# A two-block transformer kernel: second attention's queries and output projection for 258 of 272 tokens, index queries for 256 with both activation halves in one matmul

## What is computed

```
T = N_META + S                                  # 16 + 256
q, k, v, qi, ki, wi = split(rms_norm(h) @ w_in) # layer 0; qi: 8 index heads of 64, wi: 8 weights
score = sum_h wi[h] * relu(qi[h] @ ki.T)        # which 64 keys a token attends to
h = h + attention(q, top 64 keys by score) @ w_o ; h = h + conv_ffn(rms_norm(h))
kv = rms_norm(h) @ w_kv_b ; q = rms_norm(h) @ w_q_b         # layer 1
h = h + rms_norm(attn(q1, k1, v) - lam * attn(q2, k2, v)) @ w_o_b
h = h + conv_ffn(rms_norm(h))                   # convolution over the token and the 2 before it
first stack's result: h[:, 16:272]
```

## Time and profile before

| | us |
|---|---|
| median of 3 runs | 1297.96 |
| lowest and highest of them | 1296.43, 1303.09 |
| the profiled execution's own time | 1296.1 |
| its span, first to last instruction | 1294.3 |
| TensorE matmuls busy | 1269.0 (98% of the span) |
| VectorE busy | 980.1 (76%) |
| ScalarE busy | 669.2 (52%) |
| GpSimd busy | 493.9 (38%) |

### The profile page before, as it was taken

The page is one execution under the profiler, slowest core; times in us unless marked ns, Lnnn a source line. Parts: engine busy times, 40 slices in busy tenths (PEclk is TensorE's granted clock), DMA queues, the critical chain, the costliest instruction groups (busy, mean ns, idle before and its releaser), DMA issues.

```text
span 1294.3 us, 26981 instructions
## 1 busy us (share of the span) xinstructions
PE 1269.0 (98%) x8902; PEld 1176.9 (91%) x8902; DVE 980.1 (76%) x1568; ACT 669.2 (52%) x1103; POOL 493.9 (38%) x454
## 2 busy tenths in 40 slices
PE   7999999999999999999999999999999999999998
PEld 6989999999999989999888898888888988888887
DVE  5686899975666668999765687799866876999553
ACT  5445555554555555656544455355444565455442
POOL 1043465541212225555321032299611102799222
PEclk9999999999999999999999999999999999999999
DMA  8731556566633316666666565666666542666762
GB/s 219 157 99 50 167 172 181 167 175 175 182 108 107 99 50 176 183 178 194 174 198 219 150 176 161 188 181 189 192 195 195 148 139 83 180 194 193 208 188 79
DMA packets 403204, 209.20 MB, mean 162 GB/s; under 512 B 20553, under 2 KB 397681, under 8 KB 403105
## 3 DMA queue, kind: packets, MB, share of 16 engines
q1 hardware_dynamic: 402016, 205.37, 55.4%
q0 software_dynamic: 784, 2.51, 0.9%
q10 hardware_dynamic: 320, 0.21, 0.1%
HBM read 206.98 MB, written 1.27 MB: 161 GB/s over the span
## 4 chain that ended last, share of the span: by engine, by line
PE 89%; DVE 6%; issue 2%; POOL 1%; ACT 1%; DMA 0%; DVEq 0%; POOLq 0%; ACTq 0%
PE bank L621 23%; PE bank L615 15%; PE bank L617 14%; PE bank L616 14%; PE bank L622 12%; DVE w_lo L2077 2%; PE bank L758 1%; PE bank L1180 1%; PE bank L1182 1%; PE bank L1181 1%; PE bank L745 1%; PE bank L717 1%; PE bank L1032 1%; PE bank L1019 1%; PE bank L1210 1%
## 5 line engine op out<-in xcount | busy, mean ns | idle before, releaser
L2077 DVE TENSOR_TENSOR w_lo<-w_raw,w_hi 128x1024 fp32r<-128x1024 f32 x391 | 514.4, 1328 | 28.6 <-ACT w_hi L1437 27.7
L1437 ACT ACTIVATE w_hi<-w_raw 128x1024 fp32r<-128x1024 f32 x391 | 410.7, 1053 | 128.9 <-PE bank L622 64.9
L615 PE MATMUL bank<-split_x,w_lo 128*128 128x272 f32 (+2 forms) x1128 | 328.8, 291 | 1.0 <-DVE split_x L2315 0.7
L617 PE MATMUL bank<-split_x,w_hi 128*128 128x272 f32 (+2 forms) x1128 | 321.9, 285 | 0.0
L616 PE MATMUL bank<-split_x,w_hi 128*128 128x272 f32 (+2 forms) x1128 | 321.8, 285 | 0.0
L621 PE MATMUL bank<-split_w,w_hi 128*128 128x512 f32 x880 | 307.0, 393 | 0.6 <-POOL split_w L1936 0.5
L622 PE MATMUL bank<-split_w,w_lo 128*128 128x256 f32 x880 | 246.2, 280 | 0.0
L615 PEld LDWEIGHTS bank<-split_x,w_lo 128*128 128x128 f32 x1128 | 211.4, 187 | 3.9 <-DVE split_x L2315 0.9
L616 PEld LDWEIGHTS bank<-split_x,w_hi 128*128 128x128 f32 x1128 | 211.8, 188 | 0.3
L617 PEld LDWEIGHTS bank<-split_x,w_hi 128*128 128x128 f32 x1128 | 211.5, 188 | 0.3
L621 PEld LDWEIGHTS bank<-split_w,w_hi 128*128 128x128 f32 x880 | 164.8, 187 | 38.0 <-POOL split_w L1936 0.8
(11 more groups left out here) (301 smaller groups left out, 1841.3 us busy)
## 6 DMA issues: line engine op xcount, KB each, us to landing
w_raw<-in_mlp_w_dram SPq DMA_DIRECT2D x256, 256.0 KB, 3.2
w_raw<-in_w_up_dram SPq DMA_DIRECT2D x176, 256.0 KB, 3.3
w_raw<-in_w_down_dram SPq DMA_DIRECT2D x64, 256.0 KB, 3.3
w_raw<-in_a_w_in_dram SPq DMA_DIRECT2D x64, 256.0 KB, 3.4
w_raw<-in_w_in_a_dram SPq DMA_DIRECT2D x32, 256.0 KB, 4.3
w_raw<-in_w_kv_b_dram SPq DMA_DIRECT2D x32, 256.0 KB, 3.1
w_raw<-in_a_w_out_dram SPq DMA_DIRECT2D x32, 256.0 KB, 3.2
w_raw<-in_w_down_dram SPq DMA_DIRECT2D x32, 192.0 KB, 4.1
```

The source lines that it names most:

```text
L615: pe.matmul(dst, lo, mov_h, start=first, stop=False)
L617: return pe.matmul(dst, hi, mov_h, start=False, stop=last)
L1437: act.activation(w_hi[:, n % R, :], w_raw[:, n % R, :], ACT.Copy)\
L2077: dve.tensor_tensor(w_lo[:, n % R, :], w_raw[:, n % R, :], w_hi[:, n % R, :].bitcast(F32), ALU.subtract)\
```

## The change

Two things are done. The queries of layer 1 and its output projection are computed for tokens 14 to 271 in place of 0 to 271: `q` tiles and `wo_b` tiles have 258 columns, and what reads them too. And tiles 1 to 5 of stage `in` (index queries and index weights) are computed for tokens 16 to 271 by `mm2`, with the halves of the bank joined by a reduction on VectorE where a copy stood.

```diff
+Q0 = CONV_IN[1]
...
-            def from_x(s, t0=0):
+            def from_x(s, t0=0, joint=None):
...
-                both = (lambda k: split_x[:, :, k, t0:T]) if s.name in HALVES else None
+                joint = s.name in HALVES if joint is None else joint
+                both = (lambda k: split_x[:, :, k, t0:T]) if joint else None
...
             for g in range(18):
-                product(s, None, g, m=8 if g == 5 else P, **from_x(s))
+                if 1 <= g <= 5:
+                    product(s, None, g, m=8 if g == 5 else P, **from_x(s, META, True))
+                else:
+                    product(s, None, g, **from_x(s))
...
-                    ins = mm3(stream[2 + j % 2][:, 0:T], w_lo[:, slot, w], w_hi[:, slot, w], mh[:, k, :],
-                              ml[:, k, :], k == 0, k == DT - 1)
+                    t0 = Q0 if kind == "q" else 0
+                    ins = mm3(stream[2 + j % 2][:, 0:T - t0], w_lo[:, slot, w], w_hi[:, slot, w],
+                              mh[:, k, t0:T], ml[:, k, t0:T], k == 0, k == DT - 1)
...
-                    ins = mm3(stream[(s.t0 + g) % R][:, 0:T], w_lo[:, (s.n0 + g) % R, w],
-                              w_hi[:, (s.n0 + g) % R, w], aoh[:, k, :], aol[:, k, :],
+                    ins = mm3(stream[(s.t0 + g) % R][:, 0:T - Q0], w_lo[:, (s.n0 + g) % R, w],
+                              w_hi[:, (s.n0 + g) % R, w], aoh[:, k, Q0:T], aol[:, k, Q0:T],
                               k == 0, k == DT - 1)
...
-                return dict(mh=lambda k: aoh[:, k, :], ml=lambda k: aol[:, k, :], t0=0,
+                return dict(mh=lambda k: aoh[:, k, Q0:T], ml=lambda k: aol[:, k, Q0:T], t0=Q0,
...
-                act.activation(query_b(2 * (c % 4) + 1, c // 4)[64:P, :], stream[2 + j % 2][64:P, 0:T],
-                               ACT.Copy)
+                act.activation(query_b(2 * (c % 4) + 1, c // 4)[64:P, Q0:T],
+                               stream[2 + j % 2][64:P, 0:T - Q0], ACT.Copy)
...
-                act.activation(sq_b[n % 2], stream[2 + j % 2][:, 0:T], ACT.Square).then_inc(b_sq, 1)
+                act.activation(sq_b[n % 2][:, Q0:T], stream[2 + j % 2][:, 0:T - Q0], ACT.Square)\
+                   .then_inc(b_sq, 1)
...
                     if g == 0:
-                        dst, src = ki, bk[:, 0:T]
-                    elif g < 5:
-                        dst, src = qi[:, g - 1, :], bk[:, 0:T]
+                        ins = dve.tensor_copy(ki, bk[:, 0:T])
                     else:
-                        dst, src = wi[0:8, :], bk[0:8, 0:T]
-                    dve.tensor_copy(dst, src).then_inc(S["tile_read"], 1)
+                        n = P if g < 5 else 8
+                        dst = qi[:, g - 1, META:T] if g < 5 else wi[0:8, META:T]
+                        ins = dve.tensor_reduce(dst, bk[0:n, :].rearrange("p (s t) -> p t s", s=2),
+                                                AX.X, ALU.add)
+                    ins.then_inc(S["tile_read"], 1)
...
-                    dve.tensor_copy(query_b(2 * (c % 4), c // 4)[0:64, :], bk[0:64, :])\
+                    dve.tensor_copy(query_b(2 * (c % 4), c // 4)[0:64, Q0:T], bk[0:64, 0:T - Q0])\
                        .then_inc(qb_half, 1)
...
-            residual_stage("wo_b", 0)
+            residual_stage("wo_b", Q0)
```

## The result

The changed kernel takes 1293.73 us in the median of 21 runs (1293.15 to 1295.32), the kernel before 1296.59 us in as many (1295.57 to 1303.09). The ratio is 0.9974, 95% interval 0.9967 to 0.9981: 2.5 to 4.3 us less. The forecast was 1294.3, and 3.7 us less. The sign came out, 3.7 us lies in the interval, and the change stayed within 0.5%. The medians, though, are 2.9 us apart and the profiled executions 2.6, about 1 us less than the forecast's sum, and that difference turned out to have a place and a cause. That the absolute time fell so near to 1294.3 is luck: the forecast started from a median of three runs, 1297.96, and the kernel before measured 1296.59 in 21, so the same sum would have given 1292.9.

A forecast was written before the change was run, and what follows sets the result against it. TensorE's matmul stream, busy 98% of the span at full clock, was taken as the bound. Terms 1.27 + 1.27 + 1.21 - 0.05 = 3.7 us, so 1297.96 - 3.7 = 1294.3 us; range 1290.8 to 1298.8.

The forecast's parts named there:

- The sign: Whole kernel: faster, 3.7 us less; the case of the gain kept in full had chance 0.70.
- The bound and the prices: TensorE's matmul stream bounds the changed stages; 125.8 ns per 272-column matmul, 119.2 ns per 258-column one.
- Index part: Stage `in`, index tiles: 40 steps from 377.4 to 347.2 ns, 1.21 us less, 0.05 of it not passed on.
- VectorE's wait at 48.72: Stage `in`: VectorE waits 1.16 us for a relu of tile 9, so at most 1.16 us of gain pass.
- Queries: Layer 1's query tiles: 192 matmuls from 272 to 258 columns, 1.27 us less, kept.
- Output projection: Layer 1's output projection: 192 matmuls from 272 to 258 columns, 1.27 us less, kept.
- GpSimd's reserve of 1.52 us: Behind the output projection: sum of squares ready 1.52 us before TensorE's sum; at least 0.25 us stays.
- The reductions: Stage `in`, VectorE: five reductions, 680 against 439 ns for a copy, 1.2 us more on VectorE, zero on the path.
- The remaining gap: Stage `in`: of VectorE's smaller idle time before a copy, some 0.7 us remain with the reduction.
- the second attention's last units: Stretch before layer 1's output projection: no term given, so zero change, with the granted clock high in all 40 slices.
- The rivals: The one with 2.5 us: index part lost in front of the first attention, 1295.5 us, chance 0.15.
- Two rivals: First attention: waits vanish, gain up to 9.0 us, chance 0.08; more VectorE-GpSimd meetings, 1.5 us each, chance 0.07.

The follow-up runs named there:

- layer 1 alone: Kernel before with only layer 1's queries and output projection at 258 columns, index tiles as before; 1296.47 us against 1297.74, ratio 0.9987.
- the repetition: The unaltered changed kernel measured and profiled once more beside the kernel before; 1294.9 us against 1297.34, ratio 0.998.
- the twelve idle matmuls: Changed kernel plus six idle matmuls in the wait at 457.33 and six ahead of the meta tokens' outputs; 1294.42 us against before's 1297.17, ratio 0.9974.
- the projection alone: Kernel before with only layer 1's output projection at 258 columns, queries and index tiles as before; 1296.75 us against 1297.34, ratio 0.9993.
- doubling: Changed kernel with the reductions of index tiles 1 to 4 done twice; 1294.55 us against before's 1297.34, ratio 0.9978.

## Why the prediction was right, point by point

**The bound and the prices.** TensorE's stream was the bound in all three places, and the spacings of 125.8 and 119.2 ns held in the output projection (125.8 and 119.3).

**Index part:** 1.13 us measured (S1), 1.16 forecast. The 0.05 that it took off for VectorE's wait at 48.72 were owed to nothing: that wait ended 1.39 us earlier (47.33) and was still 1.77 us long. Without them 1.21 was the price, 0.08 too much: a step took 349 ns (twenty of them from 19.86 to 26.84) in place of 347.2, and 40 x (377.4 - 349) = 1.14.

**Queries:** 1.09 in the whole change, 1.13 in layer 1 alone and in the repetition, 1.27 forecast. The term was mis-sized by 0.14 to 0.18 us, 5.7 to 5.9 ns a matmul in place of 6.6. The price came from an undisturbed stream, and these tiles are cut in two by other small matmuls. The profiles show where the rest went: the first matmul behind each such interruption takes as long in either width (402.51 to 402.74 before, 405.07 to 405.29 after; 0.22 us in the mean of all), and only the others went from 126.0 to 119.6 ns. Of 192, some 176 are others: 176 x 6.4 = 1.13 us.

**Output projection:** 1.27 forecast. Counted from its first matmul (470.53 before) to the sum of squares it took 28.48 us before, 27.20 with layer 1 alone and 27.22 with the twelve idle matmuls: 1.28 and 1.26 less. The 1.47 of S4 in the whole change hold a wait of 0.22 us in front of that first matmul as well, which went because TensorE, at half clock, came later; with the projection alone (1.14) it went too, and 0.3 us turned up behind the first products instead. GpSimd's reserve of 1.52 us shrank to 0.66; the forecast said it would stay above 0.25.

**The reductions** cost TensorE nothing, by the profile and by doubling. The remaining gap was 0.62 to 0.97 us; the prediction had some 0.7.

**What failed** is the zero that the prediction gave, without naming it, to the second attention's last units: that the clock stays high. It said that the granted clock was in its top tenth in all slices, and went on as if that could not move with the program. The half clock lengthened this stretch by 1.42 us, of which 0.2 came back in the wait. Measured for measured: 1.13 + 1.09 + 1.27 = 3.5 us of shorter stream, 1.2 lost to the clock, and 0.26 + 0.07 us of scatter in parts that nothing touched make the profiled difference of 2.6. In the three stretches a queries' term 0.18 too large and a wait of 0.2 that went cancel, so that their 3.7 agree with the forecast's 3.7 better than the terms do. The rivals had 2.5 us too, for the wrong reason: there the index part was to be lost in front of the first attention. Two rivals told of waits in the first attention; they stayed as they were, 4.2 us in 8 pieces, and the meetings of VectorE and GpSimd with them (0.52 and 1.37 us at the same two places).

**What stays open:** the profiles show where the clock fell in one execution each; of the others only its mean is on record. By the means a fall somewhere is in at least 21 of 32 executions of the changed kernel, and in at least 29 of 90 of the kernel before, where it may lie elsewhere. The fastest runs, 2.3 and 2.4 us apart and not 3.7, say the same. Why the clock falls in one execution and not in another of the same program, and why the change made it more frequent, is not shown.

## What to carry to other kernels

Where TensorE is never idle, columns taken off a matmul are worth their spacing, read from long stretches of either width, and the part of the chain behind should be checked for whoever has the smallest reserve. But a part of the program in which TensorE waits or runs tiny matmuls can lose its clock in some executions, and a change elsewhere can make that more frequent. Look at the granted clock of such stretches by the microsecond and not by the slice of the page, before and after, and at the mean clock of every run: executions with the same clock can be compared where medians over a mixture can't. Judge a gain below 0.5% by lengths between fixed points of the profile, part by part. S1, S2 and S4 repeated to 0.05 us in profiles of the same kernel, where medians of a dozen runs do not; the long rest differed by 0.7.

## What the runs showed of the hardware that was not expected

The granted clock at the end of the second attention was 1.00 in the kernel before and fell to its lower level for 3.4 us in the changed one, with the same instructions in that stretch and the same waits ahead of it (0.85 and 1.05 us). With all behind the first attention shifted by 1.0 us it was 10.2 us in the profiled execution, while three of that kernel's eleven executions had a mean clock of 0.999 and no such fall. Taking four idle matmuls out of that stretch of the kernel before left the clock at 1.00. While the clock is low a group of four 272-column matmuls takes 1.12 us in place of 0.74. The page's line of granted clocks has a 9 there in both kernels: 3.4 us are a tenth of a slice. The first matmul of 272 or of 258 columns behind a run of small ones took 0.22 us of the stream in either width, the next ones 0.126 and 0.120.
